# Hybrid layers: one block from the mixture to the next layer's first projections, and one block for the start

## The reference, cut to what matters

```
for l in range(2):
    h = rmsnorm(x, norm1_g[l])
    # splits of h @ w_in[l]: inputs of three branches, and mgate
    g = sigmoid(mgate)                          # one gate per branch and feature
    m = g0 * (y_hg @ w_br_hg) + g1 * (y_gla @ w_br_gla) + g2 * (y_nsa @ w_br_nsa)
    x = x + m @ w_out[l]
    h = rmsnorm(x, norm2_g[l])
    x = x + (silu(h @ w_gate[l]) * (h @ w_up[l])) @ w_down[l]      # 1024 -> 2816 -> 1024
x = rmsnorm(x, final_norm_g)
```

## Time and profile before

| | before |
|---|---|
| median of 3 runs | 2412.97 us |
| profiled execution | 2406.2 us, span 2404.4 us |
| TensorE busy | 2098.0 us (87%) |
| VectorE busy | 1455.8 us (61%) |
| ScalarE busy | 1037.7 us (43%) |
| mean granted TensorE clock | 0.914 |
| moved by DMA | 371.73 MB, mean 155 GB/s |

### The profile page before, as it was taken

One profiled execution on the slowest core, in us unless ns is written; L12 is line 12 of the kernel. 1 busy time (PEld: TensorE's weight loads), 2 busy tenths in 40 slices (PEclk: granted clock), 3 DMA queues, 4 the chain that ended last, 5 costly groups with the idle time before them and its releaser, 6 DMA issues. The chain is left out here.

```text
span 2404.4 us, 40251 instructions
## 1 busy us (share of the span) xinstructions
PE 2098.0 (87%) x16890; PEld 1989.7 (83%) x16890; DVE 1455.8 (61%) x2309; ACT 1037.7 (43%) x1444; POOL 0.2 (0%) x4
## 2 busy tenths in 40 slices
PE   4879798799869787987999677999979898899997
PEld 4878777699868787776999667999979876799997
DVE  3757555578658575555887564655548755555554
ACT  3643433344336433434443333444446544444443
POOL 0000000000000000000000000000000000000000
PEclk8989889899989897998999888999989997899999
DMA  4333423489843334233998322555534421445552
GB/s 171 123 106 106 125 75 109 140 286 314 302 145 115 97 115 132 71 114 131 317 328 292 121 81 77 178 184 180 182 113 150 149 80 44 140 149 179 182 183 97
DMA packets 101124, 371.73 MB, mean 155 GB/s; under 512 B 11344, under 2 KB 11600, under 8 KB 100560
## 3 DMA queue, kind: packets, MB, share of 16 engines
q1 hardware_dynamic: 99936, 363.90, 46.0%
q10 hardware_dynamic: 1008, 5.26, 0.6%
HBM read 368.07 MB, written 1.05 MB: 154 GB/s over the span
## 5 line engine op out<-in xcount | busy, mean ns | idle before, releaser
L292 DVE TENSOR_TENSOR low<-raw,high 128x1024 fp32r<-128x1024 f32 x594 | 725.9, 1223 | 566.4 <-ACT high L289 565.5
L355 PE MATMUL ps<-hh,high 128*128 128x256 f32 x3248 | 942.6, 290 | 87.7 <-PEq L585 59.4
L356 PE MATMUL ps<-hh,low 128*128 128x256 f32 x3248 | 925.9, 285 | 0.0
L357 PE MATMUL ps<-hl,high 128*128 128x256 f32 x3248 | 924.5, 285 | 0.0
L289 ACT CAST high<-raw 128x1024 fp32r<-128x1024 f32 x594 | 620.7, 1047 | 641.5 <-PE ps L357 604.2
L355 PEld LDWEIGHTS ps<-hh,high 128*128 128x128 f32 x3248 | 638.0, 196 | 108.1 <-issue 99.6
L356 PEld LDWEIGHTS ps<-hh,low 128*128 128x128 f32 x3248 | 636.1, 196 | 0.6 <-issue 0.5
L357 PEld LDWEIGHTS ps<-hl,high 128*128 128x128 f32 x3248 | 635.8, 196 | 0.0
L356 PE MATMUL ps<-hidden_high_half,low 128*128 128x256 f32 x512 | 143.0, 279 | 0.0
L355 PE MATMUL ps<-hidden_high_half,high 128*128 128x256 f32 x512 | 142.9, 279 | 0.0
L357 PE MATMUL ps<-hidden_low_half,high 128*128 128x256 f32 x512 | 142.6, 279 | 0.0
(11 more groups left out here) (386 smaller groups left out, 2735.8 us busy)
## 6 DMA issues: line engine op xcount, KB each, us to landing
raw<-in_stream SPq DMA_DIRECT2D x594, 512.0 KB, 3.7
ada_rows<-in_ada SPq DMA_DIRECT2D x96, 512.0 KB, 5.0
bias<-in_bias ACTq DMA_DIRECT2D x1, 1536.0 KB, 7.3
xT<-in_xT ACTq DMA_DIRECT2D x1, 1024.0 KB, 3.9
c_act<-in_c SPq DMA_DIRECT2D x2, 512.0 KB, 4.4
out<-xT SPq DMA_DIRECT2D x1, 1024.0 KB, 3.9
par<-in_par ACTq DMA_DIRECT2D x1, 910.0 KB, 12.9
hybrid_const<-in_const ACTq DMA_DIRECT2D x1, 800.0 KB, 9.8
```

The source lines that it names most:

```text
L292: return dve.tensor_tensor(self.low[:, slot, :], self.raw[:, slot, :], self.high[:, slot, :].bitcast(F32), ALU.subtract)
L355: pe.matmul(out, sh, mh, start=start, stop=False, **more)
L356: pe.matmul(out, sl, mh, start=False, stop=False, **more)
L357: return pe.matmul(out, sh, ml, start=False, stop=stop, **more)
```

## The change

The engines' lists of mixture rest, mixture halves, output product, norm, hidden product and down product stand in one block (`feed_forward`), and for layer 0 it goes on with the next layer's norm and first four projections. The start is one block too: first splits, first norm, first projections; par1 of both layers is loaded there, const1 and par3 (final_1 and the ada biases, formerly in par2) later in it, and par2 in the block of the final norm.

`Entry` does a norm inside a block. The gained but not yet normalized tiles are rounded and split as the residual pairs come (tiles uh, ul); the first four pairs of the following product take these and their results are multiplied by the row of the reciprocal deviation on VectorE. The sums of squares are one-column matmuls with the squares as the stationary side, the deviation is worked out on a column, and a matmul spreads it to a row. Meanwhile hh and hl are made from normalized tiles for the later pairs. The mixture's halves and the hidden tensor are waited for pair by pair. Of the adaLN rows, 24 (from the third set of four hidden units on) go beside the hidden product and 24 beside the 22 units of the down product, and SyncE's list has a unit's transfer before the row's.

```diff
+                if ready is not None and k % 2 == 0:
+                    ready(pe, k // 2)
...
+        def first_loads(sp):
+            for i in range(RING):
+                ring.load(sp, i, i)
+            for i in range(RING):
+                sp.wait_ge(ring.split.sem, i + 1)
+                ring.load(sp, RING + i, i)
+        def first_parameters(act):
+            act.dma_start(xT[:, :, :], x_in).then_inc(x_loaded, 16)
+            for l in range(DEPTH):
+                act.dma_start(par1[:, l, :], par1_in[l, :, :]).then_inc(x_loaded, 16)
+            act.dma_start(const[:, :], const_in[:, 0:N_KEPT]).then_inc(loaded, 16)
+            act.dma_start(lb[:, :], lb_in).then_inc(loaded, 16)
...
+        IN_SWIGLU = 24
...
+            def sync(self, sp):
+                for i in range(self.n):
+                    self.w.sync(sp, [i])
+                    if self.mods is not None:
+                        self.mods.sync(sp, self.rows(i))
...
+            def rows(self, i):
+                return IN_SWIGLU + (i + 1) * (ADA - IN_SWIGLU) // self.n
...
+            def weigh(self, dve, n):
+                c = n % (KD // 2)
+                if n >= 2:
+                    dve.wait_ge(*self.at(split_x, KD, n - 1))
+                for m in range(2):
+                    k, to = 2 * c + m, self.staged[:, n % 2, m, :]
+                    if n < KD // 2:
+                        ins = dve.tensor_scalar(to, xT[:, k, :], self.gain[:, k:k + 1], None, ALU.mult)
+                    else:
+                        ins = dve.scalar_tensor_tensor(to, xT[:, k, :], self.gain[:, k:k + 1], self.row, ALU.mult, ALU.mult)
+                tell(ins, weighed)
+            def round(self, act, n):
+                c = n % (KD // 2)
+                act.wait_ge(*self.at(weighed, KD, n + 1))
+                tell(act.copy(self.halves(n)[0][:, 2 * c:2 * c + 2, :], self.staged[:, n % 2, :, :]), rounded_x)
+            def split(self, dve, n):
+                c = n % (KD // 2)
+                xh, xl = self.halves(n)
+                dve.wait_ge(*self.at(rounded_x, KD, n + 1))
+                tell(dve.tensor_tensor(xl[:, 2 * c:2 * c + 2, :], self.staged[:, n % 2, :, :],
+                                       xh[:, 2 * c:2 * c + 2, :].bitcast(F32), ALU.subtract), split_x)
+            def early(self, pe, c):
+                pe.wait_ge(*self.at(split_x, KD, c + 1))
...
+            def add_sums(self, pe, c):
+                pe.wait_ge(*self.at(squares, KD // 2, c + 1))
+                for k in (2 * c, 2 * c + 1):
+                    for t in range(TT):
+                        ins = pe.matmul(ps[:, 4 + t, 0:1], sq[:, k, t * P:(t + 1) * P], ones[:, 0:1], start=(k == 0),
+                                        stop=(k == KD - 1), skip_group_check=True)
+                if c == KD // 2 - 1:
+                    tell(ins, summed)
+            def spread(self, pe):
+                pe.wait_ge(*self.at(rstd_column, 1, 1))
+                for t in range(TT):
+                    ins = pe.matmul(ps[:, 6, t * P:(t + 1) * P], first_halves[:, 2, t:t + 1].broadcast_to([P, P]), ident,
+                                    start=True, stop=True)
+                tell(ins, rstd_row)
...
+            def column(self, dve):
+                dve.wait_ge(*self.at(summed, 1, 1))
+                tell(dve.tensor_scalar(first_halves[:, 0, :].unsqueeze(2), ps[:, 4:4 + TT, 0:1], 1.0 / D, EPS, ALU.mult, ALU.add), variance)
+                dve.wait_ge(*self.at(deviation, 1, 1))
+                tell(dve.reciprocal(first_halves[:, 2, :], first_halves[:, 1, :]), rstd_column)
+            def take_row(self, dve):
+                dve.wait_ge(*self.at(rstd_row, 1, 1))
+                InOrder(dve, dve_step)(dve.tensor_copy(self.row, ps[:, 6, 0:T]))
...
+            def tensor(self, pe, res, product):
+                for j in range(KD // 2 if res is not None else 0):
+                    res.tensor(pe, j)
+                    if j:
+                        self.add_sums(pe, j - 1)
+                u = (self.uh, self.ul)
+                product(pe, 0, u, 0, self.early)
+                if res is None:
+                    pe.wait_ge(loaded, 16 * 2)
+                    for c in range(KD // 2 - 1):
+                        self.add_sums(pe, c)
+                self.add_sums(pe, KD // 2 - 1)
+                product(pe, 0, u, 1, None)
+                self.spread(pe)
+                for j in range(1, EARLY):
+                    product(pe, j, u, None, None)
...
+                    act.wait_ge(x_loaded, 16 * (1 + DEPTH))
+                act.activation(first_halves[:, 3, :], xT[:, 0, 0:TT], ACT.Square)
+                for j in range(KD // 2):
+                    if res is not None:
+                        res.scalar(act, j)
+                    else:
+                        first_round(act, j)
+                    self.round(act, j)
+                    square_tiles(act, j)
+                self.deviation(act)
+                c = KD // 2
+                self.round(act, c)
+                product(act, 0)
+                self.round(act, c + 1)
+                product(act, 1)
+                if res is None:
+                    bounds_exponentials(act)
+                    late_parameters(act)
+                self.round(act, c + 2)
+                self.round(act, c + 3)
...
+            def vector(self, dve, res, product):
+                for j in range(KD // 2):
+                    if res is not None:
+                        units = list(res.prod.units_of(j))
+                        for i in units[:-1]:
+                            res.unit(dve, i)
+                        res.add(dve, j)
+                        res.prod.after_read(dve, j)
+                    else:
+                        first_split(dve, j)
+                        if j == 0:
+                            dve.wait_ge(x_loaded, 16 * (1 + DEPTH))
+                    self.weigh(dve, j)
+                    if res is not None:
+                        res.unit(dve, units[-1])
+                    self.split(dve, j)
+                if res is None:
+                    bounds_differences(dve)
+                if res is not None and res.mods is not None:
+                    res.mods.finish(dve)
+                self.column(dve)
+                self.take_row(dve)
+                c = KD // 2
+                self.weigh(dve, c)
+                product(dve, 0)
+                self.weigh(dve, c + 1)
+                self.split(dve, c)
+                product(dve, 1)
+                if res is None:
+                    bounds_logarithms(dve)
+                self.weigh(dve, c + 2)
+                self.split(dve, c + 1)
+                self.weigh(dve, c + 3)
+                self.split(dve, c + 2)
+                product(dve, 2)
+                self.split(dve, c + 3)
+                product(dve, 3)
...
-        IN_SWIGLU = 32
...
+        def round_mix(act, j):
+            act.wait_ge(mixed.sem, mixed.base + j + 1)
+            tell(act.activation(mh[:, 2 * j:2 * j + 2, :], (hk, hog)[j // 2][:, j % 2 * 2:j % 2 * 2 + 2, :],
+                                ACT.Copy, scale=0.5), mix_rounded)
+        def split_mix(dve, j):
+            dve.wait_ge(mix_rounded.sem, mix_rounded.base + j + 1)
+            tell(dve.scalar_tensor_tensor(ml[:, 2 * j:2 * j + 2, :], (hk, hog)[j // 2][:, j % 2 * 2:j % 2 * 2 + 2, :], 0.5,
+                                          mh[:, 2 * j:2 * j + 2, :].bitcast(F32), ALU.mult, ALU.subtract), mix_split)
...
+            def rows(i, u):
+                return min(max(3 * (i - 2) + min(u, 2) + 1, 0), IN_SWIGLU)
...
+                    mix.sync(sp)
+                    out.sync(sp)
                     for i in range(w.n):
-                        mods.sync(sp, min(i // 4 * 3 + min(i % 4, 2), IN_SWIGLU))
                         w.sync(sp, [i])
+                        mods.sync(sp, rows(i // 4, i % 4))
+                    down.sync(sp)
+                    if proj is not None:
+                        proj.sync(sp)
                 @block.tensor
                 def _(pe):
-                    for j in range(KF):
-                        prod.tensor(pe, h, j)
+                    for p in mine:
+                        mix.tensor(pe, p)
+                    entry.tensor(pe, out, lambda pe, j, x, only, ready: prod.tensor(pe, x, j, only, ready))
+                    for j in range(EARLY, KF):
+                        prod.tensor(pe, h, j, None, entry.late if j == EARLY else None)
+                    if proj is not None:
+                        entry2.tensor(pe, down, lambda pe, j, x, only, ready:
+                                      proj.early_tensor(pe, projected[j], x, only, ready))
+                    else:
+                        for j in range(KD // 2):
+                            down.tensor(pe, j)
+                            if j:
+                                add_squares(pe, j - 1, 1)
+                        add_squares(pe, KD // 2 - 1, 1)
...
```

(30 more changed lines are left out.)

428 lines of the change are left out of this document (237 added, 191 removed).

## The result

The changed kernel took 2394.15 us (median of 4 runs, 2392.43 to 2398.61), beside 2413.93 (4 runs) for the kernel before: ratio 0.992, 95% interval 0.990 to 0.994. It is faster, but by 20 us and not by 53.3; the range's upper end (2386) was too low.

What follows compares the result with a forecast made beforehand. TensorE's products (87% busy) set the time, leaving its idle and low-clock time to win. 8 + 14.4 + 19.6 + 17.3 + 3 - 9 = 53.3 us off 2413 gave 2359.7, stated as 2359; own range 2350 to 2368, with rivals 2338 to 2386.

Steps and rivals of the forecast that it cites:

- A: Start, up to the first block's end: ends at 56 to 57 us instead of 64.7, a gain of 8 us.
- B: Mixture to output product: idle 6.98 us and low clock go, a stall of 1.3 comes; gain 7.2 us a layer.
- C: Output product, norm, gate and up: idle 10.12 us and 2.5 of clock go; gain 9.8 us a layer.
- D: FFN hidden to down product: idle time, low clock and layer 0's 2.02 us stall go; gain 17.3 us.
- E: Layer 0's down product, norm and next projections: gain kept at 3 us, despite added adaLN rows paced by transfers.
- F: Layer 1's down product: more adaLN rows, paced by transfers, make VectorE finish later; loss of 9 us.
- rival 1: Down products: transfers keep up, ends come 8 us (layer 0) and 7 us (layer 1) sooner; 2344 us, chance 0.17.
- par2 loaded during the final norm: Final norm: 0.86 MB, about 4.5 us, beside the norm's 7 us; costed at nothing, 4.5 us if uncovered.
- hidden and mixture halves in other tiles: Hidden and mixture halves: their move to other tiles was costed at nothing.
- rival 2: Hand-overs of B and C cost more: stalls followed by low clock, late halves 3 us later; 14 us, 2373, chance 0.21.
- Rival 3: SyncE's queue in the FFN: row-unit cycle over about 3.65 us loses the gain; 2430 us at 3.8, chance 0.03.
- rival 4: Half of B to D stays, as engines in one block still wait in the same order; 2385 us, chance 0.07.

Runs made afterwards that it cites:

- s_start: The changed kernel with all four first units rounded and split before the first pair of x is weighed; 2385.97 us, ratio 0.9891 to the kernel before.
- a_hh256: The changed kernel with 56 unused words ahead of xT and 8 behind lb, restoring hh's old place modulo 256; 2366.21 us, ratio 0.9805.
- d_notransfer: The changed kernel without transfers of each layer's last 24 adaLN rows, VectorE doing the same work on old data; 2368.89 us, ratio 0.9816.
- r_rows: The changed kernel with six adaLN rows a layer moved beside the mixture, leaving the down product's last four units none; 2372.95 us, ratio 0.9836.

## Why the prediction was wrong

**A, the start, was mis-sized and is the first step that failed: 0.3 of 8 us.** The trace gives three terms. I let the first rounding start at 7.99, with x and the parameters there by then; they were there at 11.15, and since a square of x stands ahead of that rounding in ScalarE's order, which I did not look at, it started at 11.27. So the fourth split ended at 27.2 and not at 24.4 (2.8). The row was copied from 41.63 on and not at 36.3 (2.5 more): the one-column sums took 6.82 us where I took 5, their records being 0.21 us apart here, near the 0.19 at a clock of 0.5 behind layer 0's down product and not the 0.10 at full clock. And VectorE's list ran for 23.4 us from there to 65.0, not 19.5, with waits of low parts for ScalarE of 1.64, 1.04 and 1.03 us (3.9). s_start removes the first term and gains 9.7 us: its fourth split ends 6.4 us sooner, since the four roundings no longer wait for x nor for one another's pair, and its sums take 4.90 us, while VectorE's list still takes 23 us.

**B held.** 6.5 us a layer for 7.2; 7.6 with the operands in place. **C held:** 10.4 and 10.7 for 9.8. **D held** in a_hh256, 11.3 and 5.9 (17.2 for 17.3); in the changed kernel 7.5 and 2.6, since each of 36 units takes 2.86 us and not 2.76.

**E and F held.** The next projections' stage gained 1.9 (3 forecast), with the forecast idle time ahead of the fourth quarter, at 11.35 somewhat longer than the 7 to 10. Layer 1 lost 9.8 (9 forecast), and d_notransfer and r_rows show it to come with the rows' transfers, so rival 1 is out. VectorE in the last units of the changed kernel:
```profile
1288.30 1.22 DVE L1845 SCALAR_TENSOR_TENSOR ada_rows<-ada_rows,c_act 128x1024 f32<-128x1024 f32 x1 [1.34 <-DMA ada_rows<-in_ada]
...
1291.52 1.23 DVE L1845 SCALAR_TENSOR_TENSOR ada_rows<-ada_rows,c_act 128x1024 f32<-128x1024 f32 x1 [0.85 <-DMA ada_rows<-in_ada]
...
1294.70 1.23 DVE L1845 SCALAR_TENSOR_TENSOR ada_rows<-ada_rows,c_act 128x1024 f32<-128x1024 f32 x1 [0.80 <-DMA ada_rows<-in_ada]
```
The cycle is 3.2 us, for the 3.13 of the earlier trace rows that the forecast took over. That bytes set it was argued in the prediction and stays so: the round trip of two buffers, above, gives the same cycle. The 425 GB/s that the Trainium skill's HBM Reference (Specifications (TRN2)) gives for one core streaming alone did not show in any stretch of 10 us of the down product that I looked at; the highest was 353, in r_rows.

**What failed most was costed at nothing: "par2 loaded during the final norm" and "hidden and mixture halves in other tiles".** I priced these moves as transfers or not at all, and left the second network out of the sum. What they changed was the place of tiles: without par2 ahead of it hh lay 6880 bytes lower, and most tiles behind it moved by other amounts. By stage, the spans of the changed kernel and a_hh256 differ by 19.1 us in the second network, 7.1 in the hidden products, 4.4 in the branches and 0.8 in the rest: 31.4. The prediction's remark that a unit's pace differs at the same clock (2.76 against 2.98), "for which I have no cause", touched on it: in the kernel before ffn_high's matmuls are 119.4 to 121.0 ns apart and hh's 115, which is about half of that difference, the sums of squares being the rest. I priced it at "a few us either way" and didn't put it into the range. With it taken out, a span of 2365.4 us stands against 2351 forecast: missing are the start (7.3) and the branches (6.9), and the small terms cancel. That the medians are closer (2366.2 for 2359, within the forecast's own range) is luck: the profiled execution of the kernel before, from which the span was forecast, was 7 us below its median.

**The branches** were taken as untouched. They cost 11.3 us more, 6.9 in a_hh256. That they follow the time at half clock is measured; why there is more of it is not settled. Rivals 2 to 4 did not occur: between mixture and down product no stall is over 1.3 us, and the only time at 1.2 GHz is the first 3.6 us, left over from the branches. Rival 3's sum counted 30 units with a row beside the hidden product where the change has 24: over 2x(24+22) units its bound would be 3.72 and not 3.65 us; the verdict on it is the same.

## What to carry to other kernels

When a change adds or removes a tile that lives ahead of others, compare the addresses of TensorE's operands before and after, and try one or two pads before judging the change: here the same schedule took 2366, 2380, 2394 and 2417 us by pads alone. A moved stage is to be read in each engine's written order: what needs a late input must not stand ahead of what doesn't. And where a stage waits for its transfers, count what is moved into it; six transfers moved out of a stage at 0.90 DMA share were worth 21 us over both layers.

## What the runs showed of the hardware

- Matmuls of 128x128 by 128x256 in this data type (fp32r), at full clock: 113.3, 116.7, 117.8, 118.3, 118.7 or 120.0 ns from start to start, by the places of the operands and, at two places, by what ran before. The lowest came only with the moving operand 64 bytes above a multiple of 256 and the weights (32896 and 49280) 128 above one.
- At such a place (84032) there are two courses, 113.3 and 117.8 ns: the first behind a stop, and behind bursts at 77184 and 77216 without one; the second straight behind bursts at 77248 and 77152. At 77216 it is 116.7 ns behind a stop and 117.8 behind a burst at 77184.
- Work of ScalarE and VectorE beside a burst changed nothing in it (120.0 and 117.8 ns with and without; not tried at a place of 113.3).
- One-column matmuls, two records each (32 for 16 matmuls), are 0.10 us a record apart at full clock and 0.19 at a clock of 0.5.
- Matmuls added to bridge a gap kept the clock up at the next stage's entry (7.32 us idle to 1.80), but the same stage fell to half clock later anyway, and the time changed by -1.8 us in one kernel (no more than noise) and rose by 6.2 in another.
